# The end of an expert stage: banks, scatter, squares, conversions and one branch rearranged

## The reference

```python
h2 = rmsnorm(x, norm2_g[l])
x = x + hierarchical_moe(h2, ...)      # 32 experts, top 2, w1, w3 and w2 per expert
...
xn = rms_norm(x, norm_mix)             # r = rsqrt(mean(x*x)); x * r * gain
proj = xn @ w_in                       # first products of the second block
```

## Time and profile before

| | |
|---|---|
| three runs | 1912.51, 1906.58, 1909.08 us; median 1909.08 |
| the profiled execution | 1905.19 us; its span 1903.6 us |
| PE busy | 1835.0 us, 96% of the span |
| DVE, ACT, POOL busy | 832.6, 584.8, 765.5 us |
| mean granted TensorE clock | 0.974 of full speed |

### The profile page before, as it was taken

One profiled execution on the slowest core, in us unless ns is written; L12 is line 12 of the kernel. 1 busy time (PEld: TensorE's weight loads), 2 busy tenths in 40 slices (PEclk: granted clock), 3 DMA queues, 4 the chain that ended last, 5 costly groups with the idle time before them and its releaser, 6 DMA issues.

```text
span 1903.6 us, 23507 instructions
## 1 busy us (share of the span) xinstructions
PE 1835.0 (96%) x8837; PEld 1361.5 (72%) x8837; DVE 832.6 (44%) x1263; ACT 584.8 (31%) x1082; POOL 765.5 (40%) x629
## 2 busy tenths in 40 slices
PE   9999979999999999999899889999999999999999
PEld 6888757775887444443688776777778878888887
DVE  4121665455443233232523576999338552202221
ACT  3223334443232111110231334555435222212221
POOL 4444423333540000000232548888825544544452
PEclk9999989999998999999899899999999999999999
DMA  6323212223333899999422322222253323233321
GB/s 224 99 79 99 78 55 84 84 84 139 106 127 137 317 352 392 338 371 374 149 88 91 125 96 95 67 67 73 71 207 111 122 77 100 91 98 100 94 95 44
DMA packets 81895, 266.36 MB, mean 140 GB/s; under 512 B 8320, under 2 KB 9344, under 8 KB 81792
## 3 DMA queue, kind: packets, MB, share of 16 engines
q1 hardware_dynamic: 61152, 224.02, 33.8%
q10 hardware_dynamic: 18336, 32.51, 4.7%
q0 software_dynamic: 2304, 8.39, 1.3%
HBM read 248.11 MB, written 16.78 MB: 139 GB/s over the span
## 4 chain that ended last, share of the span: by engine, by line
PE 89%; DVE 6%; ACT 2%; DMA 1%; issue 1%; ACTq 1%; POOL 0%; SPq 0%; POOLq 0%; DVEq 0%
PE psum L560 86%; DVE root L1888 1%; PE psum L900 1%; PE psum L1238 1%; ACTq L1794 1%; DVE area L1904 1%; DMA more<-stream 1%; PE psum L674 1%; DVE area L2430 1%; DVE area L1963 1%; PE psum L868 0%; ACT area L1385 0%; ACT root L1385 0%; DVE yt_lo L2211 0%; ACT ring_hi L1385 0%
## 5 line engine op out<-in xcount | busy, mean ns | idle before, releaser
L560 PE MATMUL psum<-area_r,ring_hi 128*128 128x512 f32 (+1 forms) x3168 | 995.1, 396 | 8.8 <-DVE area_r L1857 2.4
L458 POOL TENSOR_TENSOR ring_lo<-ring,ring_hi 128x512 fp32r<-128x512 f32 x436 | 584.9, 1364 | 898.8 <-ACT ring_hi L1385 893.8
L560 PEld LDWEIGHTS psum<-area_r,ring_hi 128*128 128x128 f32 x3168 | 591.6, 190 | 146.8 <-issue 21.4
L560 PE MATMUL psum<-area_r,ring_lo 128*128 128x512 f32 (+1 forms) x1584 | 617.7, 390 | 0.0
L1385 ACT ACTIVATE ring_hi<-ring 128x1024 fp32r<-128x1024 f32 x218 | 229.8, 1057 | 610.9 <-PE psum L560 559.9
L560 PEld LDWEIGHTS psum<-area_r,ring_lo 128*128 128x128 f32 x1584 | 300.2, 190 | 62.4
L1385 ACT ACTIVATE area<-psum 128x512 f32<-128x512 f32 (+3 forms) x256 | 124.2, 512 | 210.0 <-PE psum L674 71.4
L1888 DVE RECIPROCAL root<-root 128x512 f32<-128x512 f32 (+1 forms) x30 | 94.1, 3137 | 134.3 <-ACT root L1385 134.3
L560 PE MATMUL psum<-area 128*64 128x128 f32 (+6 forms) x832 | 112.1, 346 | 14.6 <-DVE area L1889 9.7
L560 PE MATMUL psum<-ring,area 128*64 128x512 f32 (+1 forms) x416 | 108.9, 619 | 0.2 <-issue 0.2
L560 PE MATMUL psum<-more,area 128*64 128x512 f32 x384 | 92.6, 604 | 8.9 <-DVE area L2206 6.7
(11 more groups left out here) (219 smaller groups left out, 1660.0 us busy)
## 6 DMA issues: line engine op xcount, KB each, us to landing
ring<-stream SPq DMA_DIRECT2D x324, 512.0 KB, 3.5
more<-stream SPq DMA_DIRECT2D x48, 1024.0 KB, 7.2
area<-gates ACTq DMA_DIRECT2D x40, 256.0 KB, 5.8
gates<-root ACTq DMA_DIRECT2D x24, 256.0 KB, 2.0
gates<-area ACTq DMA_DIRECT2D x16, 256.0 KB, 2.8
area<-xT SPq DMA_DIRECT2D x8, 256.0 KB, 4.5
area<-xT ACTq DMA_DIRECT2D x8, 256.0 KB, 3.6
tokens<-area ACTq DMA_DIRECT2D x2, 1024.0 KB, 4.2
```

Source lines behind the costliest of these rows:

```text
L458: ins = nc.gpsimd.tensor_tensor(ring_lo[:, c % RS, n], ring[:, c % R, n], ring_hi[:, c % RS, n].bitcast(F32), ALU.subtract)
L560: return nc.tensor.matmul(out, lhsT, rhs, start=first, stop=last)
```

## The change

1. *Banks of its own for the last pair.* `second` of group 3, pair 3 writes to banks 0 and 7 (`LAST2`), no longer to 3 and 4, and doesn't wait for `yt_lo` of the pair ahead of it. Its rounding on ACT and subtraction on DVE are made in two halves of 512 columns.
2. *Staged scatter.* In group 3 `turn(3,3)` stands ahead of `unit(3,15)`, and DVE's `turned(3,3)` ahead of `low(3,2)`. The last scatter goes to banks 5, 6, 1, 2, 4, 7, 5, 6 (`LASTX`); pair 2's part of m = 0..3 is issued ahead of the wait for pair 3.
3. *Squares added by three engines.* POOL adds squared tiles 0 to 3 into one, DVE adds 4 and 5, and 6 and 7; TensorE makes 3 token sums and not 8.
4. *Conversions moved up.* `selT1` and `more0` change places. ACT loads the root's table and converts chunks MOE1 and MOE1+1 ahead of the rounding of pair 2, MOE1+2 and MOE1+3 ahead of that of pair 3. POOL subtracts for MOE1 and MOE1+1 ahead of its adds, for the other two behind them.
5. *TensorE's branch turned.* `gathered` is the first arm, `dense` the second; both have the sums and `spread_rstd(2)` within (`nx_sums`).

```diff
-        selT = [... offset=high_at + 4 * 512 * (NT + x * PAIRS))
+        selT = [... offset=high_at + 4 * 512 * (NT + 2 * x * PAIRS))
-            (high_at + 4 * 512 * (NT + 2 * PAIRS), area_at + 2048 * XT, area_at + 2048 * (XT + 4)))]
+            (high_at + 4 * 512 * (NT + PAIRS), area_at + 2048 * XT, area_at + 2048 * (XT + 4)))]
+        LAST2 = (0, 7)
+        LASTX = (5, 6, 1, 2, 4, 7, 5, 6)
...
-            split(MOE1, CMP0)
+            pool.wait_ge(weights_used, MOE1 - 4)
+            low(split_no(MOE1) + 1, MOE1)
+            low(split_no(MOE1 + 1) + 1, MOE1 + 1)
+            for n, (a, b) in enumerate(((0, 1), (2, 3), (0, 2))):
+                pool.wait_ge(S("normsq"), KD * NB["nx"] + max(a, b) + 1)
+                if n == 2:
+                    pool.wait_ge(S("consts2"), 6)
+                nc.gpsimd.tensor_tensor(tile(Q2 + a), tile(Q2 + a), tile(Q2 + b), ALU.add).then_inc(S("consts2"), 1)
+            pool.wait_ge(S("sp_x"), KD * 2 * GROUPS)
+            low(split_no(MOE1 + 2) + 1, MOE1 + 2)
+            low(split_no(MOE1 + 3) + 1, MOE1 + 3)
+            for c in range(MOE1 + RS, CMP0):
+                low(split_no(c) + 1, c)
...
+            def nx_sums():
+                pe.wait_ge(S("consts2"), 7)
+                token_sums(tile(Q2), 0, False)
+                pe.wait_ge(S("sq_sum"), KD - 2 + 1)
+                token_sums(tile(Q2 + 4), 4, False)
+                pe.wait_ge(S("sq_sum"), KD - 2 + 2)
+                token_sums(tile(Q2 + 6), 6, True).then_inc(S("normsum"), 1)
+                spread_rstd(2)
...
-                    if g or p:
+                    if (g or p) and not last:
                         pe.wait_ge(S("sp_yl"), g * PAIRS + p)
...
-                    unit(g, 15)
+                    if g < GROUPS - 1:
+                        unit(g, 15)
                     turn(g, PAIRS - 1)
+                    if g == GROUPS - 1:
+                        unit(g, 15)
                     second(g, PAIRS - 1)
+                def last_scatter(p, m):
+                    for x, t in enumerate((yt_hi, yt_lo)):
+                        ins = mm(psum[:, LASTX[m], :], t[:, p, P * m:P * m + P], selT[g % 2][:, p, :],
+                                 p % 2 == 0 and x == 0, p % 2 == 1 and x == 1)
+                    return ins
+                pe.wait_ge(S("sp_yl"), PAIRS * g + PAIRS - 1)
+                for m in range(4):
+                    if m < 2:
+                        pe.wait_ge(S("sp_x"), KD * 2 * g + KD - 1 + m)
+                    last_scatter(PAIRS - 2, m)
                 for m in range(KD):
-                    scatter(GROUPS - 1, 1, m)
+                    if m % 4 == 0:
+                        pe.wait_ge(S("sp_yl"), PAIRS * GROUPS + m // 4)
+                    if m >= 6:
+                        pe.wait_ge(S("sp_x"), KD * (2 * g + 1) + m - 5)
+                    if m >= 4:
+                        last_scatter(PAIRS - 2, m)
+                    last_scatter(PAIRS - 1, m).then_inc(S("sp_s"), 1)
+                nx_sums()
...
-            with pe.If(crowded == 1):
-                dense()
-            with pe.Else():
-                gathered()
-            for k in range(KD):
-                pe.wait_ge(S("normsq"), KD * NB["nx"] + k + 1)
-                ins = token_sums(tile(Q2 + k), k, k == KD - 1)
-            ins.then_inc(S("normsum"), 1)
-            spread_rstd(2)
+            with pe.If(crowded == 0):
+                gathered()
+            with pe.Else():
+                dense()
...
+                preload(ACT.Sqrt, 5)
+                act.wait_ge(S("sp_t"), PAIRS * GROUPS)
+                high(MOE1)
+                high(MOE1 + 1)
+                high_pair(g, 2)
+                act.wait_ge(S("sp_s"), KD * 2 * g)
+                high(MOE1 + 2)
+                high(MOE1 + 3)
+                act.wait_ge(weights_used, MOE1)
+                for x in range(2):
+                    A(yt_hi[:, PAIRS - 1, 512 * x:512 * x + 512], psum[:, LAST2[x], :], ACT.Copy).then_inc(S("sp_yh"), 1)
...
+            for k in (4, 6):
+                dve.wait_ge(S("normsq"), KD * NB["nx"] + k + 2)
+                V.tensor_tensor(tile(Q2 + k), tile(Q2 + k), tile(Q2 + k + 1), ALU.add).then_inc(S("sq_sum"), 1)
```

More of the change, by code:

```diff
@@ L1014, in second @@
                 def second(g, p):
+                    last = g == GROUPS - 1 and p == PAIRS - 1
                     pe.wait_ge(S("sp_hT"), g * PAIRS + p + 1)
@@ L1025, in second @@
                                 s0 = SLOTS * ex
-                                ins = mm(psum[s0:s0 + SLOTS, 3 + half, :], hT[p % 2][:, f, s0:s0 + SLOTS],
+                                ins = mm(psum[s0:s0 + SLOTS, LAST2[half] if last else 3 + half, :], hT[p % 2][:, f, s0:s0 + SLOTS],
                                          w[ex][:, 512 * half:512 * half + 512], f == 0, f == FE - 1)
@@ L1619, in gathered @@
                 rows_even(1, 1)
-                high(0, 1)
+                high_pair(0, 1)
                 rows_even(1, 2)
@@ L1623, in gathered @@
                 silu(0, 3)
-                high(0, 2)
-                high(0, 3)
+                high_pair(0, 2)
+                high_pair(0, 3)
                 for g in range(1, GROUPS):
@@ L1646, in gathered @@
                     silu(g, 3)
-                    high(g, 2)
-                    high(g, 3)
+                    if more:
+                        high_pair(g, 2)
+                        high_pair(g, 3)
+                g = GROUPS - 1
+                preload(ACT.Sqrt, 5)
+                act.wait_ge(S("sp_t"), PAIRS * GROUPS)
+                high(MOE1)
+                high(MOE1 + 1)
+                high_pair(g, 2)
+                act.wait_ge(S("sp_s"), KD * 2 * g)
[4 more added lines that the diff above has]
+                    A(yt_hi[:, PAIRS - 1, 512 * x:512 * x + 512], psum[:, LAST2[x], :], ACT.Copy).then_inc(S("sp_yh"), 1)
             def dense():
@@ L1658, in dense @@
                             A(root[:, f, :], psum[:, 4 * (n % 2) + 2 * f, :], ACT.Silu).then_inc(S("fb_silu"), 1)
+                preload(ACT.Sqrt, 5)
+                for c in range(RS):
+                    high(MOE1 + c)
             act.wait_ge(S("flag_ok"), 1)
@@ L1667, in _ @@
             used[0] = MOE1
-            def loads2():
-                for c in range(RS):
-                    high(MOE1 + c)
-            norm("nx", lambda k: tile(X + k), lambda k: tile(Q2 + k), then=loads2,
+            norm("nx", lambda k: tile(X + k), lambda k: tile(Q2 + k),
                  ready=lambda k: act.wait_ge(S("sp_x"), KD * (2 * GROUPS - 1) + k + 1))
@@ L2209, in low @@
                 def low(g, p):
+                    if g == GROUPS - 1 and p == PAIRS - 1:
+                        for x in range(2):
+                            dve.wait_ge(S("sp_yh"), PAIRS * GROUPS + x)
+                            c = slice(512 * x, 512 * x + 512)
+                            V.tensor_tensor(yt_lo[:, p, c], psum[:, LAST2[x], :], yt_hi[:, p, c].bitcast(F32),
+                                            ALU.subtract).then_inc(S("sp_yl"), 1)
+                        return
                     dve.wait_ge(S("sp_yh"), g * PAIRS + (p + 1))
@@ L2217, in scattered @@
                         dve.wait_ge(S("sp_s"), KD * (2 * g + half) + m + 1)
-                        V.tensor_tensor(tile(X + m), tile(X + m), psum[:, 5 + m % 2, :], ALU.add).then_inc(
-                            S("sp_x"), 1)
+                        bank = LASTX[m] if (g, half) == (GROUPS - 1, 1) else 5 + m % 2
+                        V.tensor_tensor(tile(X + m), tile(X + m), psum[:, bank, :], ALU.add).then_inc(S("sp_x"), 1)
                 rows_odd(0, 0)
@@ L2280, in gathered @@
                     scattered(g, 0, 2, 6)
+                    if not more:
+                        turned(g, 3)
                     low(g, 2)
                     scattered(g, 0, 6, 8)
-                    turned(g, 3)
+                    if more:
+                        turned(g, 3)
                 low(GROUPS - 1, 3)
```

11 lines of the change are left out of this document (6 added, 5 removed).

## The result

| | before | changed |
|---|---|---|
| median of 7 runs | 1909.08 us | 1893.26 us |
| lowest, highest | 1906.58, 1912.94 | 1889.26, 1899.86 |
| ratio, 95% interval | | 0.9915 [0.9896, 0.9935] |
| the profiled execution, its span | 1905.19, 1903.6 | 1894.97, 1893.4 |

The change made the kernel 15.8 us faster (12.4 to 19.9 by the interval).

A forecast was written before the change was run, and what follows sets the result against it. TensorE, 89% of the chain, was taken to bound the kernel by waits and thin token sums. Terms -1.7 - 2.4 - 4.6 - 0.6 = -9.3 us gave 1895.9 us profiled, 1899.8 for the median; range 1895.5 to 1906.

The forecast's parts named there:

- Turn ahead of unit 15: End of the last group: `second(3,3)` starts when the eight scatter matmuls end, at 908.6 not 910.30: -1.7 us.
- Last scatter: TensorE's 2.41 us wait before the last scatter is filled with eight matmuls of pair 2; both edits together -4.1 us.
- (a): Last scatter's need: `yt_lo` of pair 2, rounded by ACT until 910.1, 2.7 us later, subtracted by DVE until 911.3.
- (b): Last scatter's need: DVE's two adds behind pair 2's subtraction, 911.3 to 912.6; TensorE wants the first at 912.3.
- (c): Last scatter's need: next two conversions done by 912.3, then pair 3's halves of `yt_lo` at 913.7 and 914.4.
- Squares: Last add to root: fewer token sums, DVE's adds at 1.37 us each, root 4.0 us behind the add: -4.6 us.
- Spread: Sums' end to first product of the second block: between 0 and -1.8 us by TensorE's clock; -0.6 taken.
- Branch, entry: TensorE's jump over the dense arm, hidden in a 3.16 us wait for gathered rows: 0, bounded by 8.3 us.
- Branch, exit: New jump behind the queued spread, about 4 us before the first product is due: 0 if under 4 us.
- The third rival: The new exit jump's fetch exceeds its cover while ACT stores x: 0 to +8 us, +5 taken, 1904.8; chance 0.08.
- ACT's line: Rival: roundings of pairs 2 and 3 come late behind four chunks: only -5 us, 1904; chance 0.12.
- the staying clock: Rival: clock stays at 1.2 GHz through `vsw`, gate records and `kv` chunks, costing 15 us: 1914.8; chance 0.05.

The follow-up runs named there:

- sq8: Changed kernel with all eight squared tiles summed by TensorE, no adds on POOL and DVE: 1900.77 us, 0.9958 of the kernel before.
- free_adds: Changed kernel with POOL's conversion of MOE1+2 held until DVE has added its two pairs of squares: 1895.31 us, 0.9937 of the kernel before.
- conv_back: Changed kernel with the four conversions and the table load back behind the squares: 1896.88 us, 0.9946 of the kernel before.
- wg_in: Changed kernel with the 32 gate matmuls moved into the time in which `vsw` waits for DVE's norm: 1893.87 us, 0.9921 of the kernel before.
- again: Changed kernel, unaltered, measured a second time: 1896.22 us, 0.9936 of the kernel before.
- scatter_only: Kernel before with only the last pair's banks, the staged scatter and the turn ahead of unit 15: 1902.89 us, ratio 0.9977.
- squares_only: Kernel before with only the squares added by POOL and DVE: 1906.39 us, ratio 0.9987.
- br_back: Changed kernel with TensorE's branch as before, dense arm first, sums and spread behind the join: 1898.78 us, 0.9945 of the kernel before.
- null: Kernel before, unaltered, measured against itself: 1909.01 us, ratio 1.0002.
- branch_only: Kernel before with only TensorE's branch turned, eight token sums and the spread inside the first arm: 1906.47 us, ratio 0.9987.

## Why the prediction was wrong, point by point

- **Turn ahead of unit 15 (-1.7): right.** `second(3,3)` starts 9.88 us behind the last `silu`, 11.68 before: -1.8.
- **Last scatter (-2.4, both -4.1): right in mechanism, a little small.** The scatter starts 13.47 us behind the `silu` instead of 17.74, -4.3, and every one of (a), (b) and (c) came within a microsecond of the times given: in terms of the `silu`, ACT's rounding of pair 2 moved by 2.5 us (2.7 predicted) and nobody waited for it. The last add ends 4.8 us earlier. I had let the 32 matmuls take their 7.9 us of before; with banks of their own they took 7.5, and the add behind the last came sooner.
- **Squares (-4.6): right.** The root stands 3.7 and 4.5 us behind the last add (4.0 predicted), -4.9 and -4.1 against before; DVE's adds took 1.3 each. `sq8` confirms the sign, `free_adds` that POOL slowed the adds. One detail was wrong: I had the first sum hidden; TensorE waited 1.11 us for POOL.
- **Spread (-0.6): within the bounds for DVE, wrong for TensorE.** Root to norm is 2.8 and 3.6 us, 3.6 before: -0.8 and 0, by how far the clock had fallen. TensorE's first product came 7.42 us behind the sums' end in the first profile and not 5.3, for the exit jump, without cost.
- **Conversions (0): right** in that and in what they cost if left (`conv_back`).
- **Branch, entry (0): this step failed.** I wrote that "taking that jump away gives 0", because the wait of 3.16 us in the earlier trace rows was a DMA's, and I took 0 out of bounds that reached to 8.3 us. Over five profiles with the old branch and nine with the new it is -1.9 us, with no overlap between the two (6.2 to 8.1 and 4.8 to 5.4 us). The Trainium skill (Runtime: NRT & Kernel Launch, "Instruction fetch mechanics"), which says that a taken branch out of the fetched pages stalls for a fetch, was cited against the new exit jump and should have been turned on the one taken away; the traces agree with it, at up to 4.11 us of idle time ended by issue, though no view shows the fetch itself.
- **Branch, exit (0): right**, though the jump was bare on TensorE for some 2.3 us in the first profile. The third rival's place and the reason why it might cost nothing both held.
- **The other rivals** fell: ACT's line wasn't late, the clock stayed full through the sums of the first profile but not through the spread, and it was back at 0.97 in the idle time behind the spread. The argument against the staying clock was misread, though: before, the clock was not full again 6 us after each fall. It was at 0.50 or falling from 928 to 936 us and still at 0.61 in 936 to 940, some 10 us; and in `wg_in` it stayed at 0.50 for some 13.

From the last `silu` to `kv` the two profiles of the changed kernel gained 10.5 and 8.5 us on that of before: -9.5 for a forecast of -9.3. That the two agree so well is in part luck, since the clock alone moves this stretch by 2 us. With the entry it makes -11.4, which lies in the interval of `again` (-9.7 to -14.7) and 1.0 us outside that of the first measurement (-12.4 to -19.9). So the failed step is the one term of the change that was wrong, but it doesn't carry the median out of the range by itself: with -1.9 for the entry the forecast would have been 1897.9 us. A second step failed beside it: carrying a profile's gain over to the median by adding 3.9 us, as if both kernels' profiled executions lay as far under their medians. The changed kernel's lay 1.7 us above.

**What stays open.** Some 1.3 and 4.4 us more were measured, in the two measurements, than these stretches show. The clock on record accounts for most of what separates the two (medians 1893.26 and 1896.22 us, means 1893.43 and 1895.80): the first seven runs had a mean clock of 0.9770, the six of `again` 0.9757, which at 1.4 us per 0.001 is 1.8 of the 2.4 us between the means. So the first measurement was lucky by about that much, and the 12.7 us of `again` are the better figure for the change. What gave those runs the higher clock isn't shown. The profiles also differ where nothing was changed: POOL's gather starts at 608.4 to 613.6 us, and from `kv` to the end it takes 937.3 and 937.7 us before and changed, but 934.2 in `again`.

A candidate for the rest: in three of the five profiles with the old branch (`scatter_only`, `squares_only`, `br_back`) the stage took 283.0 to 287.7 us and not 281.0 to 281.7, with the clock lower behind the branch. TensorE and its clock for 10 to 20 us behind its first transposes, in `br_back` and in the changed kernel (stretch, length, PE, clock, DMA share, GB/s):

```profile
628.76:638.76 10.00, 10.00 (x38) 0.69 0.34 118
```

```profile
627.13:637.13 10.00, 9.75 (x55) 1.00 0.76 274
```

None of the nine profiles with the new branch shows it. If it comes with the late entry it is worth some 2 us on average, but `before` and `null` had the late entry without it, three out of five is few, and `branch_only`'s -1.5 us leaves little room for it.

## What to carry to other kernels

A wait in one profiled execution names the releaser that came last in that execution. Where two are within a microsecond or two of each other (here a gather and a jump), look at several profiles, and price the edit by the other one too, before calling it hidden. Before looking for the cause of a difference between two medians, compare the mean granted clocks of their runs: here 0.001 went with 1.4 us. And a small edit ahead of a fall of the clock can't be read from one profile, since the fall comes earlier or later by more than the edit is worth (`free_adds`). Work of many small matmuls ahead of a root is a place to save that no list of waits shows, and parts of a change that uncover each other (fewer sums, earlier conversions) have to be taken together.

## What the runs showed of the hardware

- A jump over a long arm on TensorE cost 1.9 us on average against falling through (five profiles and nine), with up to 4.11 us of idle time put down to issue; the same sort of jump at the exit let TensorE start 0.15 to 2.49 us behind its data in eight profiles, and one put ahead of a wait showed nothing at all.
- Sums on one column ran 64 records in 9.44 us in one kernel and 11.65 in another. The clock fell to 1.2 GHz behind more than 4 us of them in the first and some 2 us in the second, in both with no idle time ahead of them.
- POOL's conversions made DVE's adds of two SBUF tiles 1.7 times as long (2.63 us for two against 1.56), and slowed DVE's norm of a tile beside them (0.69 to 1.63 us for its second part in `conv_back`).
- Runs of one kernel differed by up to 12.0 us (`scatter_only`, 1900.52 to 1912.51), more than any single part of this change, and the time went with the mean granted clock (0.975 and 0.969 in these two).
